# Neighbourhood attention: the value product of the item two steps back moved to the head of a step

## The reference

```python
qb = q_row.reshape(b, n_cb, NA_COL_BLOCK, h, d)
sc = jnp.einsum('bjqhd,bkjchd->bhjqkc', qb, k_band).astype(jnp.float32) * scale
sc = jnp.where(mask, sc + bias.astype(jnp.float32), -jnp.inf)
p = jax.nn.softmax(sc, axis=(-2, -1)).astype(v.dtype)
o = jnp.einsum('bhjqkc,bkjchd->bjqhd', p, v_band)
...
o_b = o_b * jax.nn.silu(g_b)
```

## Time and profile before

| what | us |
|---|---|
| median of 3 runs | 1868.63 |
| lowest and highest | 1867.83, 1869.66 |
| span of the profiled execution | 1865.4 |
| median of the runs less that span | 3.2 |
| PE busy in the span | 1830.1 (98%) |
| the four pairs' step loops | 396 to 430, 458 to 502, 524 to 570, 590 to 617 of the span |

### The profile page before, as it was taken

How to read it: one execution, slowest core, us unless ns; L and a number is a source line. 1 busy time by engine, 2 the same in 40 slices (tenths; PEclk the granted TensorE clock), 3 DMA queues, 4 the chain that set the end, 5 groups by cost and what they waited for, 6 DMA issues and landing times.

```text
span 1865.4 us, 37306 instructions
## 1 busy us (share of the span) xinstructions
PE 1830.1 (98%) x15533; PEld 1483.5 (80%) x15533; DVE 950.1 (51%) x2056; ACT 793.7 (43%) x1725; POOL 412.2 (22%) x415
## 2 busy tenths in 40 slices
PE   9999999999999999999999999999999999999998
PEld 8997766888887789877877878778787886667887
DVE  5677766233444354135555565555653357775523
ACT  5346666343444433224343343433432346655421
POOL 5650000111112431222222222222221301101221
PEclk9999999999999999999999999999999999999999
DMA  5153310234323333330221221212213220005442
GB/s 192 47 172 90 86 40 1 97 96 140 106 88 111 114 124 94 114 110 32 82 63 60 69 64 59 72 56 77 64 43 98 88 81 19 1 1 181 149 156 90
DMA packets 146000, 159.81 MB, mean 86 GB/s; under 512 B 15093, under 2 KB 123961, under 8 KB 145833
## 3 DMA queue, kind: packets, MB, share of 16 engines
q1 hardware_dynamic: 145800, 157.37, 26.4%
q0 software_dynamic: 32, 0.07, 0.0%
HBM read 110.53 MB, written 52.62 MB: 87 GB/s over the span
## 4 chain that ended last, share of the span: by engine, by line
PE 93%; ACT 3%; DVE 2%; POOL 1%; issue 1%; DMA 0%; DVEq 0%; POOLq 0%; ACTq 0%
PE ps L998 9%; PE ps L696 7%; PE ps L1000 7%; PE ps L999 7%; PE ps L697 7%; PE ps L698 7%; PE ps L1109 4%; PE ps L811 3%; PE ps L790 3%; PE ps L890 3%; PE ps L1146 3%; PE ps L892 3%; PE ps L891 3%; PE ps L798 3%; PE ps L1295 3%; PE ps L1318 2%
## 5 line engine op out<-in xcount | busy, mean ns | idle before, releaser
L2820 POOL TENSOR_TENSOR t<-t,t 128x512 fp32r<-128x512 f32 x183 | 238.4, 1316 | 848.0 <-ACT t L1422 828.2
L998 PE MATMUL ps<-t,t 128*128 128x512 f32 (+2 forms) x720 | 291.0, 404 | 1.5 <-POOL t L2820 1.5
L696 PE MATMUL ps<-t,t 128*128 128x256 f32 (+2 forms) x872 | 282.3, 324 | 1.7 <-ACT t L1429 1.0
L697 PE MATMUL ps<-t,t 128*128 128x256 f32 (+2 forms) x872 | 276.5, 317 | 0.0
L698 PE MATMUL ps<-t,t 128*128 128x256 f32 (+2 forms) x872 | 276.4, 317 | 0.0
L1000 PE MATMUL ps<-t,t 128*128 128x512 f32 (+2 forms) x720 | 268.3, 373 | 0.0
L999 PE MATMUL ps<-t,t 128*128 128x512 f32 (+2 forms) x720 | 267.7, 372 | 0.0
L696 PEld LDWEIGHTS ps<-t,t 128*128 128x128 f32 x872 | 165.7, 190 | 18.3 <-issue 6.9
L698 PEld LDWEIGHTS ps<-t,t 128*128 128x128 f32 x872 | 165.7, 190 | 10.4
L697 PEld LDWEIGHTS ps<-t,t 128*128 128x128 f32 x872 | 165.9, 190 | 10.2 <-issue 0.4
L998 PEld LDWEIGHTS ps<-t,t 128*128 128x128 f32 x720 | 135.8, 189 | 30.0 <-issue 7.7
(11 more groups left out here) (278 smaller groups left out, 3285.5 us busy)
## 6 DMA issues: line engine op xcount, KB each, us to landing
t<-in_w_in SPq DMA_DIRECT2D x53, 512.0 KB, 5.9
zgate_spill<-t SPq DMA_DIRECT2D x20, 512.0 KB, 3.0
tile_bias<-t SPq DMA_DIRECT2D x16, 576.0 KB
t<-tile_bias SPq DMA_DIRECT2D x8, 1152.0 KB, 5.8
t<-zgate_spill SPq DMA_DIRECT2D x16, 512.0 KB, 4.1
feat_spill<-t SPq DMA_DIRECT2D x13, 512.0 KB, 3.2
tile_bias<-band_bias SPq DMA_DIRECT2D x48, 128.0 KB
t<-values_and_gates SPq DMA_DIRECT2D x96, 64.0 KB
```

Of the source, the lines that this page charges most:

```text
L696: e.matmul(dst, lh, rh, start=k == 0, stop=False)
L697: e.matmul(dst, lh, rl, start=False, stop=False)
L998: e.matmul(dst, lh, rh, start=k == 0, stop=False)
L2820: e.tensor_tensor(WLO[wslot(b)][:, o], WST[:, o], WHI[wslot(b)][:, o].bitcast(F), ALU.subtract).then_inc(w_lo.sem, w_lo.up((b, p)))
```

## The change

On PE and on ACT the call `band_value(m - 2)` moves to the head of step n. The order on PE becomes value(m - 2), scores(m), [part of the output product], turn(m - 1), [values and gates]; on ACT value(m - 2), turned(m - 1), prob(m, 0), prob(m, 1), and so on. DVE, POOL and SP keep their programs.

```diff
@@ PE's program
                 for n in range(8):
                     m = B_Z + 8 * p + n
+                    if n > 1:
+                        band_value(m - 2)
                     band_scores(m)
                     if p == 3 and n == 3:
                         bank_at(("wo1", 0, 0), 7, (resid_v, (0, 0)))
...
                     if n:
                         band_turn(m - 1)
-                    if n > 1:
-                        band_value(m - 2)
                     if p < 3:
                         values_and_gates(p + 1, n, hi, lo, (7,))
```

## The result

The changed kernel takes 1896.8 us (median of 4 runs, 1895.7 to 1898.0), the kernel before 1868.3 in the same session (4 runs, 1867.8 to 1869.7): 28.5 us more, ratio 1.0152, interval 1.0137 to 1.0166. The forecast was 1895.6.

A forecast was written before the change was run, and what follows sets the result against it. PE, busy 98% of the span, was taken to bound the kernel. First three pairs 15.3 us plus last pair 11.7 made 27.0, added to 1868.6 for 1895.6 us; range 1883 to 1906.

The forecast's parts named there:

- The place and the releaser of the wait: PE's gate transpose at L874, n = 3 to 7 of p < 3, waits near 1.1 us for DVE's `band_output`.
- The price of a step, p < 3: Steps n = 3 to 7 of the first three pairs: period 6.56 us against 5.52, +1.04.
- First term: First three pairs: fifteen waiting steps cost 15.6 us, less 0.1 at three n = 2 steps; 15.3, bounds 13 to 18.
- ACT at nothing: ACT's moved gate copy (0.28 us) costs nothing, covered by PE's 2.85 us product.
- The last pair: Second term, p = 3: a loop closes between PE and DVE; 11.7 us, ends 8.6 and 17.9.
- POOL's share: Last pair: `band_gates` slowed beside POOL, at worst 1.1 us in each step, 6.6 extra at the top.
- The rule of the Trainium skill: Weight loads drawn ahead would save up to 0.14 us in some 20 waiting steps, 2.8 in all; left out.
- The 3.2 us above the span: Median of the runs over the profiled span of 1865.4, put down to launch and drain, untouched by the change.
- (b): Rival: the last pair gives nothing up, as DVE sets its pace; only the first term, 1883.9; chance 0.08.
- (a): Rival: clock stays down through the last pair; 33.2 us more, 1901.8, up to 1908 with POOL; chance 0.19.
- (c): Rival: gaps pull the clock down in the first three pairs too; 39 us more, 1934; chance 0.05.
- (d): Rival: bank 6 already free at the step border; order gains 0.1 us in 18 steps, 1866.6; chance 0.05.

The follow-up runs named there:

- e3: Changed kernel, but DVE runs the output of item m - 2 ahead of its gate product in step n: 1877.4 us.
- e1: Changed kernel with the new order only in head pairs 0 to 2, the order of before in pair 3: 1883.2 us.
- e5: Changed kernel with ACT's two lines taken back, so only PE has the new order: 1896.6 us.
- e2: Changed kernel with the new order only in the last head pair, p = 3: 1878.0 us.
- e7: Kernel before with the new order and e3's DVE order in the first three pairs, the last pair as before: 1865.4 us.
- e8: e7 plus seven idle matmuls in PE's gaps at n = 1 of the last pair: 1864.7 us.
- e6: Changed kernel plus 16 idle matmuls in PE's gaps at n = 1 and 2 of the last pair: 1893.2 us.

## Why the prediction was right, step by step

- **The place and the releaser of the wait.** Bank 6, held until `band_output(m - 3)`, which DVE runs behind its gate product: shown by the waits after (20, by L2230) and by e3, in which only the place of that output changed and the fifteen waits went.
- **The price of a step, p < 3: +1.04 forecast, 1.09 measured** (6.60 or 6.61 in place of 5.52). The wait in the PE row is 1.06. What was off is the gate transpose after a wait with the switch behind it, 1.06 instead of 1.01. First term 15.3 forecast, 16.2 in the trace; in e1 15.8 in the trace and 15.6 by the medians.
- **ACT at nothing:** e5, 28.4 against 28.5, each known to some 1.4. In the first three pairs nothing speaks against it. In the last pair the moved copy took 0.7 us off a step at the lower clock, as the profile of e5 shows, and that is not in the forecast.
- **The last pair: 11.7 forecast, 11.9 in the trace; in e2 11.4 in the trace and 10.4 by the medians.** The first gates ended at 614.10 with DVE's L2224 at 1.37 us beside POOL, as in the earlier trace rows; then step 2 and one more at half clock, as forecast, and 5.09, 5.10 and 4.76 where it had 5.03, 5.03 and 4.6. Two things in it were luck. That two slow steps was the right number was a choice between the bounds, not something the rows gave: the profile of e5 has it down in 624 to 627 too (0.55, against 0.95 in the changed kernel), and in e2 it came and went. And the price of a slow step was 0.2 too high, 1.55 against the 1.3 that the trace shows. The working took the half-clock start of the scores, 600.20, from a gate transpose that began at 598.38, while the new one could begin at 598.16, as the full-clock sum next to it has it. The quick steps came out 0.06 to 0.16 longer than forecast and the gate transpose of the first slow one started 0.14 behind the gates, not 0.06, which made up for most of it.
- **POOL's share** in `band_gates` was kept as an upper end. It was not needed: after the 1.37 at 612.73 L2224 takes 0.29 us in every step of the loop, since POOL's parts (1.26 to 1.42 us each) no longer run beside it: in the slow steps they lie where DVE waits for PE (from 614.12 and 621.21), later also beside its first addition, which takes 0.56 as ever.
- **The rule of the Trainium skill** (TensorE: Matmul & The Clock Gate, "Architectural detail: the array is 16× 32×32, not 1× 128×128") that PE's queue can draw weight loads ahead of matmuls in flight. The forecast read the earlier trace rows as disagreeing with it, and that was too much. At the waits of the trace after, no matmul was in flight any more, and in PE's program the wait stands ahead of the load as well as of the matmul; the load at L874 began at 413.43, 0.01 ahead of its matmul, after 1.26 us of idle time ended by DVE. Where PE doesn't wait, the load begins ahead while the matmuls before it run, as the page says (473.49 against the gate transpose at 473.60 in the trace before). To leave the 2.8 us out was right for these waits; no run here has the load ahead of its wait, so what that would give is not shown.
- **The 3.2 us above the span.** They are not all launch and drain. Every run here is 1.8 longer than its span (1898.0 and 1896.2 in the changed kernel's profile); so the profiled execution of the kernel before must have been 1.4 faster than the median, which gives the rest. The sum is the same for it.
- **The rivals.** (b), the last pair free, falls by e2 (10.4). (a), the clock down all through, falls by the windows: 1.00 from 630 on. (c) falls: no first pair lost the clock, with PE stopping for 1.06 of 6.6 us. (d) happened only in the first pairs of e3, e7 and e8, where the DVE order made it true.

What was off is the size of (d)'s gain: 0.19 us a step, not 0.1. The forecast took the 0.08 between transposes and product; the other 0.1, of which it had no row, is that the gate transpose follows the product's last matmul sooner than the scores do, which the wait hides in the changed kernel and e3 and e7 show. So e7 came out 2.8 us below the kernel before and not 1 to 2.

## What to carry to other kernels

Moving a group to the head of a step moves its waits there too: look for what frees its PSUM bank, and where that instruction stands in its own engine's queue, behind what. If it stands behind work that needs the very product that PE has just issued, the wait is the whole chain of the other engines, here 1.1 us, and 0.74 us of other PE work in front takes 0.74 off it. The cure is to move the releaser ahead of that work, and to leave the old order where another engine sets the pace, as a loop closes there.

## Not expected of the hardware

- A gate transpose that starts after a wait holds PE 0.06 us longer than one in a running stream (0.26 to the next start in place of 0.20, 413.44 and 413.70 against the earlier trace rows), at each of the waits at the full clock. No run tried why.
- The order of PE's groups has a price of its own: five groups in the order gate transpose, value, scores, transposes, product take 5.33 us, the same five in the order scores, transposes, gate transpose, value, product 5.52, with no wait in either.
- A granted clock at the lower level costs only what of PE's work lies on the chain at that time: in the last pair of the changed kernel 1.3 us a step (value product and scores), in e6 at 620 to 624 nothing (output product and transposes), in e7 next to nothing (its last pair is 0.2 us longer than that of e8, where the clock stayed up).
